# A modulation matrix on the matrix engine, retention scores of two heads in one go, and roots spread by row tiles

## The chip, the core and the metric

The kernel runs on one core of a Trainium2 chip. Five engines work side by side, each with its own queue of instructions, and meet at semaphores: TensorE (PE, with its weight loads shown as PEld), VectorE (DVE), ScalarE (ACT), GpSimd (POOL) and SyncE (SP), which here only issues transfers. 16 DMA engines move the data. The metric is the device time of the core in microseconds (us), as the median of repeated runs.

## The reference

Two transformer blocks are run on one sequence of 256 tokens with 1024 features, all in float32. What matters here:

```python
# block 1
mod = silu(c) @ w_ada + b_ada                      # c: 1024, w_ada: 1024 x 6144
sh1, sc1, g1, sh2, sc2, g2 = mod                   # six rows of 1024
h = rms_norm(x, norm1_g) * (1.0 + sc1) + sh1
u_val, u_gate, q, k, v, f_logit, gate_c, gate_a = split(h @ w_in)
conv_out = conv_module(u_val, u_gate, ...)         # 31 taps over time, 512 channels
attn = forgetting_attention(q, k, v, f_logit)      # uses cumsum(log_sigmoid(f_logit))
...                                                # mix, then 32 experts, 4 a token
# block 2, two layers
q_a, k_a, v_a, q_r, k_r, v_r, g_f, g_b, gate_logits = split(x @ w_in_2)
y_attn = windowed_gqa(q_a, k_a, v_a) @ w_o_attn    # 8 heads
# retention, 8 heads, key size 32, value size 64, forward and backward in time
y_ret = (silu(g_f) * head_norm(y_f) + silu(g_b) * head_norm(y_b)) @ w_o_ret
merged = sigmoid(g1) * y_attn + sigmoid(g2) * y_ret
...                                                # layer 0: dense FFN, layer 1: 8 experts
```

`head_norm` takes mean and variance over the 64 values of each head and direction, so a token has 16 roots per layer.

## The kernel before

Everything on the chip is kept with features on the 128 partitions and the 256 tokens (T) along the free side: `X` and `H` are 8 tiles (KT) of 128 x 256. `Z` (38 tiles of T columns), `SQ` and `SCR` (the end of `W`) are scratch. PSUM has 8 banks of 512 float32, `ps(b, ...)` is a part of bank b.

Weights come through a stream of slots of 1 MB each (`plan`, L70 to 125): in block 1 a ring of 15 buffers. SP issues the slots in the order of the stream (L444) and waits before each until the buffer's former content is used. `Linear` names a matrix and its number of slots; `lin_done` counts its finished groups, `job_evac` says which engine copies a job's result out of PSUM. Jobs use banks 0 and 1 in turn, and a job waits until the job two before it is copied out (`bank_free`).

The opening. ACT issues the small loads, then the tokens `x`. PE turns the tokens by transposes (L767), ACT squares them into `XSQ` (L1407) and copies them into `X` (L1409); PE sums the squares over the features with eight matmuls by a matrix of ones (L774); DVE and ACT make the root from it. Meanwhile DVE makes the modulation: for each of the eight slots of `ada0` (one slot is 128 rows of `w_ada` by 2048 columns) it multiplies the slot by the column `CSIL[:, s]` and adds it to `ADA` (`ada_products`, L1780 and L1783). PE then sums `ADA` over its partitions, with 16 matmuls of one column (`ada`, L724), and DVE adds the bias into `MOD` (L1788). DVE makes the gain `GS` and the modulated `H` in four pairs of tiles, `h_ready`. Then PE runs the projections `uqkv_a` (4 jobs) and `uqkv_b` (6 jobs), L662 and L714, with `ada(1)` between them, then the forget logits (L795) and `ada(2)`. In the stream two slots of `ada1` or `ada2` follow each of the first eight projection slots. ACT copies the projections out (L1432); ahead of that it issues four small loads (L1421 to L1424: forget weights, two routers, forget bias), of which PE's forget job waits for all. DVE makes the products of `ada1`, then `CONV_IN` and the first 15 of the 31 taps of the convolution (L1833, L1836) behind the products of `ada2`, then the log-sigmoid and running sum of the forget logits, `NEGF` (L1849). PE's jobs of the projection `gates` are each followed by attention scores (`scores1`, L814 to L823), which need `NEGF`, and DVE does the other 16 taps two at a time between them.

A layer's gate stage in block 2 (`mixer2`). Weights and inputs are split in two parts, hi and lo, which ACT (L396) and POOL (L400) make; a job is three passes, 96 instructions (L651). There are 12 gate jobs `gg`. After each of the first eight, PE does one head's share of the other work: in even steps the attention scores of two heads (`scores2`, L1178), in every step the retention scores of one head (`ret_scores`, L1190), then values and transposes (L1204, L843, L832). A head's retention keys and queries take 32 partitions, so each of its matmuls uses one row tile of the array; its bank is 2. ACT copies the gate job out (L1579, from the fifth on L1602), makes the decay factors and the exponentials, copies the transposed probabilities and splits a slot of weights. DVE weights the retention scores with the decay (L2219, `ret_weighted`).

After the gate jobs comes the head norm: sums by head (`head_sums`, L1233), the squares' sums into 16 rows by `HEADROW` (L1245), the 16 roots, and their spread over the 64 values of each head by `SPREAD` (L1255), which POOL builds (L596 to L600) once the last retention head is weighted. DVE multiplies bank by bank (L2255) and adds both directions (L2257).

The lines that the steps of the argument turn on:

```python
for name, n, ada in (("uqkv_a", 4, "ada1"), ("uqkv_b", 6, "ada2")):      # stream
    for s in range(n):
        stream.append((name, s))
        stream += [(ada, k) for k in range(min(2 * s, 8), min(2 * s + 2, 8))]
...
pe.wait_ge(sem("negf_ready"), 1)                                         # scores1(0)
...
def bank_free(job):
    if job >= 2:
        e, c = job_evac[job - 2]
        pe.wait_ge(sem("evac_" + e), c)
```

## Time and profile before

| | |
|---|---|
| median of 3 runs | 2409.09 us (2408.94 to 2410.05) |
| profiled execution, its own time | 2402.67 us |
| profiled execution, span | 2400.7 us |
| PE busy | 2273.2 us, 95% of the span |
| DVE, ACT, POOL busy | 735.9, 621.7, 385.2 us |

An engine's busy time is the time in which it worked on at least one instruction. A float32 matmul is two instructions in the trace. In a timeline a row with "x64" stands for 64 instructions, one after the other, with the time from the first one's start to the last one's end. In brackets stands the idle time of the engine before them and what ended it. ACTq and SPq are the queues of ACT and SP while they issue transfers. PEclk is the granted clock of PE as a share of its full speed, 2.4 GHz; its other level is 1.2 GHz.

### The profile page before, as it was taken

The page shows a single profiled execution, that of the slowest core. Times are in us where ns is not written, and L with a number is a line of the kernel's source. Part 1 is how long each engine was busy: PE and PEld are TensorE (multiplying, and loading weights), DVE is VectorE, ACT ScalarE, POOL GpSimd, SP SyncE. Part 2 cuts the span into 40 slices and gives each one's busy share as a digit, 9 for nine tenths or more (in the row PEclk, how much of TensorE's full clock was granted, in tenths as well). Part 3 has the DMA queues.
Part 4 walks back from the last instruction along what each step waited for, and adds up shares of the span by engine and source line. Part 5 has one row for each costly group of instructions (what it writes and reads, how often), then busy time and mean ns, then how long its engine had stood idle before and what let it go on. Part 6 is the DMA issues. An engine that isn't in the chain of part 4 may idle for free.

```text
span 2400.7 us, 34716 instructions
## 1 busy us (share of the span) xinstructions
PE 2273.2 (95%) x13090; PEld 1407.5 (59%) x13091; DVE 735.9 (31%) x1369; ACT 621.7 (26%) x901; POOL 385.2 (16%) x355
## 2 busy tenths in 40 slices
PE   5999899999999999999997999999999989999897
PEld 4887744444444444444446988899898863333333
DVE  6854322222222222222235234312314341111013
ACT  1143111111111111111214761443368011111111
POOL 1000000000000000000004741688486000000000
PEclk8999899999999999999998999999999989999999
DMA  9962389999999999989993433565454366999651
GB/s 371 370 233 101 95 341 418 418 418 417 418 417 418 417 418 417 418 341 414 418 393 106 158 106 105 163 190 180 119 176 124 122 249 260 362 405 396 278 234 72
DMA packets 226472, 688.61 MB, mean 287 GB/s; under 512 B 31386, under 2 KB 120418, under 8 KB 190562
## 3 DMA queue, kind: packets, MB, share of 16 engines
q1 hardware_dynamic: 221776, 685.82, 74.5%
q10 hardware_dynamic: 4626, 1.81, 0.3%
q8 instruction: 50, 0.82, 0.1%
q14 instruction: 20, 0.16, 0.0%
HBM read 686.53 MB, written 1.05 MB: 286 GB/s over the span
## 4 chain that ended last, share of the span: by engine, by line
PE 73%; DMA 10%; SPq 8%; DVE 4%; issue 1%; ACT 1%; ACTq 1%; POOL 0%; DVEq 0%; POOLq 0%
PE PS L992 16%; PE PS L651 12%; PE PS L662 11%; DMA RAW<-in_w_exp_in 9%; PE PS L1094 7%; SPq L453 6%; PE PS L1105 4%; PE PS L956 4%; PE PS L1287 3%; PE PS L975 2%; PE PS L706 1%; PE PS L748 1%; SPq L475 1%; PE PS L1003 1%; PE PS L1052 1%
## 5 line engine op out<-in xcount | busy, mean ns | idle before, releaser
L992 PE MATMUL PS<-RAW,Z 128*64 128x512 f32 x3168 | 713.7, 597 | 23.2 <-DMA RAW<-in_w_exp_in 23.2
L400 POOL TENSOR_TENSOR WLO_D<-W,WHI_D 128x512 fp32r<-128x512 f32 x284 | 361.8, 1310 | 1193.1 <-ACT WHI_D L396 1164.3
L992 PEld LDWEIGHTS PS<-RAW,Z 128*64 128x64 f32 x3168 | 213.7, 137 | 454.4 <-issue 376.7
L1094 PE MATMUL PS<-W,Z 128*64 128x512 f32 (+1 forms) x1056 | 212.8, 558 | 11.3 <-DMA W<-in_moe_w 10.6
L662 PE MATMUL PS<-Z,W 128*128 128x256 f32 x768 | 172.2, 385 | 2.1 <-DVE Z L1900 1.5
L396 ACT ACTIVATE WHI_D<-W 128x2048 fp32r<-128x2048 f32 x71 | 135.3, 1908 | 119.4 <-DMA W<-in_ffn_w 47.6
L1094 PEld LDWEIGHTS PS<-W,Z 128*64 128x64 f32 x1056 | 75.1, 137 | 149.1 <-issue 128.2
L662 PEld LDWEIGHTS PS<-Z,W 128*128 128x128 f32 x768 | 147.6, 193 | 25.2 <-DVE Z L1900 1.9
L956 PE MATMUL PS<-Z 128*128 128x64 f32 x1088 | 128.6, 278 | 0.0
L956 PEld LDWEIGHTS PS<-Z 128*128 128x128 f32 x1088 | 127.4, 196 | 0.3 <-issue 0.3
L2021 DVE TENSOR_TENSOR Z<-Z,PS 128x1024 f32<-128x1024 f32 x66 | 80.4, 1218 | 125.9 <-PE PS L975 125.9
L662 PE MATMUL PS<-H,W 128*128 128x256 f32 x512 | 116.1, 388 | 2.4 <-ACT Z L1432 2.4
L1515 ACT ACTIVATE Z<-PS 128x512 f32<-128x512 f32 x33 | 19.7, 597 | 367.1 <-PE PS L992 367.1
L651 PE MATMUL PS<-XHI,WHI_D 128*128 128x256 f32 x784 | 111.7, 285 | 1.4 <-POOL WLO_D L400 1.4
L1105 PE MATMUL PS<-W,Z 128*64 128x512 f32 x484 | 111.1, 599 | 0.0
L651 PE MATMUL PS<-XHI,WLO_D 128*128 128x256 f32 x784 | 110.1, 283 | 0.0
L651 PE MATMUL PS<-XLO,WHI_D 128*128 128x256 f32 x784 | 110.0, 283 | 0.0
L2047 DVE COPY Z<-PS 128x512 f32<-128x512 f32 x33 | 22.8, 692 | 280.0 <-PE PS L992 280.0
L662 PEld LDWEIGHTS PS<-H,W 128*128 128x128 f32 x512 | 98.8, 195 | 16.6 <-issue 2.9
L651 PEld LDWEIGHTS PS<-XHI,WHI_D 128*128 128x128 f32 x784 | 100.7, 191 | 3.1 <-POOL WLO_D L400 2.0
L651 PEld LDWEIGHTS PS<-XLO,WHI_D 128*128 128x128 f32 x784 | 101.1, 192 | 0.0
L651 PEld LDWEIGHTS PS<-XHI,WLO_D 128*128 128x128 f32 x784 | 101.1, 192 | 0.0
(384 smaller groups left out, 2333.8 us busy)
## 6 DMA issues: line engine op xcount, KB each, us to landing
RAW<-in_w_exp_in SPq DMA_DIRECT2D x256, 1024.0 KB, 19.3
RAW<-in_w_exp_out SPq DMA_DIRECT2D x128, 1024.0 KB, 21.8
W<-in_moe_w SPq DMA_DIRECT2D x128, 704.0 KB, 15.8
W<-in_w_in SPq DMA_DIRECT2D x52, 1024.0 KB, 5.9
W<-in_moe_w SPq DMA_DIRECT2D x40, 1024.0 KB, 16.1
W<-in_ffn_w SPq DMA_DIRECT2D x33, 1024.0 KB, 5.3
W<-in_w_ada SPq DMA_DIRECT2D x24, 1024.0 KB, 14.0
W<-in_w_out SPq DMA_DIRECT2D x12, 1024.0 KB, 5.1
```

Of the source, the lines that this page charges most:

```text
L396: eng.activation(hi, raw, ACT.Copy).then_inc(sem("dense_hi"), 1)
L400: i = eng.tensor_tensor(lo[:, c:c + 512], raw[:, c:c + 512], hi[:, c:c + 512].bitcast(F32), ALU.subtract)
L453: sp.dma_start(dst, src).then_inc(sem(f"raw{s}"), 16)
L651: mm = pe.matmul(ps(job % 2, T, c0=j * T), w[:, k, c:c + P], xp[:, k, :], start=(i == k == 0), stop=(i == 2 and k == KT - 1))
L662: mm = pe.matmul(ps(job % 2, T, c0=j * T), w[:, k, c:c + P], x[:, k, :], start=(k == 0), stop=(k == nk - 1))
L956: mm = pe.matmul(ps(2, HALF, c0=k * HALF), HT[:, a, k * P:(k + 1) * P], PICK[:, a, 0:HALF], start=(a == 0), stop=(a == 1))
L975: mm = pe.matmul(ps(6 + h, T, c0=j * T), YS1[64 * h:64 * h + 64, c:c + P], GT[64 * h:64 * h + 64, :], start=True, stop=True)
L992: mm = pe.matmul(ps(bank, 512, 64 * h, 64 * h + 64), x, w[:, c:c + 512], start=first, stop=final, skip_group_check=True)
L1094: mm = pe.matmul(o if b < 2 else o.rearrange("p (i n) -> p i n", i=2), X1[:, s, :], rhs, start=(s == 0), stop=(s == 7), skip_group_check=True)
L1105: mm = pe.matmul(ps(3, 512, 64 * h, 64 * h + 64), x, second2(j)[:, c:c + 512], start=(i == j == 0), stop=(j == 5), skip_group_check=True)
L1287: mm = pe.matmul(ps(j // 2, T, c0=(j % 2) * T), w[a][:, i, j * P:(j + 1) * P], x[:, i, :], start=(s == n == i == 0 and j % 2 == 0), stop=( ...
L2021: dve.tensor_tensor(o, o, PS[:, 6:8, :].rearrange("p h (k t) -> p h k t", k=2), ALU.add)\
```

## The change

1. The order of the stream and the split of the projections: `uqkv_a` has 6 slots and jobs, `uqkv_b` 4. One slot of `ada1` follows each of the first four projection slots, two each the next two; the slots of `ada2` follow the last four, two each.
2. `ada0` is multiplied on PE: for each slot four matmuls with `CSIL[:, s]`, broadcast to 32 columns, as weights, each into its own 32 partitions of bank 0 (four column tiles). DVE copies the result to SBUF, PE turns it with four transposes, DVE adds the bias. DVE's products of `ada0` go.
3. DVE first adds the eight squared tiles to two, and PE sums these with two matmuls into bank 3 instead of eight into bank 4.
4. The four small loads are issued by POOL, not ACT.
5. DVE does seven taps before `ada(1)` and eight after the products of `ada2`.
6. Gate jobs 0 to 8 all use one bank, so each from the second on waits for the copy of the job just before it. The freed bank holds the retention scores of the odd heads, and a pair's scores are computed together, in two row tiles, in the even steps. Job 9 waits until all heads are weighted.
7. `HEADROW` has 128 columns, so that the 16 sums (and roots) stand four times, at partitions 0, 32, 64 and 96. The spread runs in four row tiles at once, in two rounds. POOL builds `SPREAD` for all four with eight selects instead of two.

```diff
-    for name, n, ada in (("uqkv_a", 4, "ada1"), ("uqkv_b", 6, "ada2")):
-        for s in range(n):
+    for name, ada, upto in (("uqkv_a", "ada1", (1, 2, 3, 4, 6, 8)), ("uqkv_b", "ada2", (2, 4, 6, 8))):
+        for s, k in enumerate(upto):
             stream.append((name, s))
-            stream += [(ada, k) for k in range(min(2 * s, 8), min(2 * s + 2, 8))]
+            stream += [(ada, i) for i in range(upto[s - 1] if s else 0, k)]
...
+        def gate_bank(l, i):
+            return (lins[f"gg{l}"].job0 + (0 if i <= 8 else i)) % 2
...
+            pool.dma_start(WF, w_in[0][:, 5 * CW:5 * CW + HEADS].rearrange("(k p) n -> p k n", p=P)).then_inc(sem("ld_small"), 16)
...
-                for half in range(2):
-                    i = pool.affine_select(out=spread[:, :, half, :], in_=spread[:, :, half, :], compare_op=ALU.not_equal,
-                                           fill=1.0, base=-half, pattern=[[-2, KT], [0, HD]], channel_multiplier=1)
+                for r in range(4):
+                    for half in range(2):
+                        o = spread[32 * r:32 * r + 32, :, half, :]
+                        i = pool.affine_select(out=o, in_=o, compare_op=ALU.not_equal,
+                                               fill=1.0, base=-half, pattern=[[-2, KT], [0, HD]], channel_multiplier=1)
...
+            def gate_job(l, i):
+                lin = lins[f"gg{l}"]
+                q = split_ready(lin, i)
+                if 1 <= i <= 8:
+                    pe.wait_ge(sem("evac_act"), job_evac[lin.job0 + i - 1][1])
+                else:
+                    bank_free(lin.job0 + i)
+                    if i == 9:
+                        pe.wait_ge(sem("ret_weighted"), HEADS * (l + 1))
+                for j in range(2):
+                    for n, (w, xp) in enumerate(PASSES):
+                        w = w[:, q % SPLIT_N, :].rearrange("p (k n) -> p k n", k=KT)
+                        for k in range(KT):
+                            mm = pe.matmul(ps(gate_bank(l, i), T, c0=j * T), w[:, k, j * P:(j + 1) * P], xp[:, k, :],
+                                           start=(n == k == 0), stop=(n == 2 and k == KT - 1))
+                mm.then_inc(sem("lin_done"), 1)
...
+            def ada_rows(s):
+                w = weights(lins["ada0"].at[s])
+                for c in range(4):
+                    mm = pe.matmul(ps(0, 512, 32 * c, 32 * c + 32), CSIL[:, s:s + 1].broadcast_to([P, 32]),
+                                   w[:, 512 * c:512 * c + 512], start=(s == 0), stop=(s == 7),
+                                   tile_position=(0, 32 * c), skip_group_check=True)
+                mm.then_inc(sem("ada_used"), 1)
+
+            pe.wait_ge(sem("cond_ready"), 1)
+            for s in range(2):
+                ada_rows(s)
             pe.wait_ge(sem("ld_x"), 16)
...
+            for s in range(2, 4):
+                ada_rows(s)
+            pe.wait_ge(sem("x_sq"), 5)
+            for k in range(2):
+                mm = pe.matmul(ps(3, T), ONES[:, :], XSQ[:, k, :], start=(k == 0), stop=(k == 1))
             mm.then_inc(sem("x_squares"), 1)
-            ada(0)
+            for s in range(4, 8):
+                ada_rows(s)
+            pe.wait_ge(sem("ada_row"), 1)
+            for j in range(4):
+                tr = pe.transpose(ps(1, P, c0=j * P), ADA[:, j * P:(j + 1) * P], IDENT[:, :])
+            tr.then_inc(sem("lin_done"), 1)
...
-                def ret_scores(h):
-                    r = (h % 4) * RK
-                    n = HEADS * l + h
+                def ret_scores(h0):
+                    n = HEADS * l + h0
                     if n:
                         pe.wait_ge(sem("ret_weighted"), n)
                     for a in range(2):
-                        k0, q0 = (KR + h // 4) * T + a * P, (QR + h // 4) * T
-                        mm = pe.matmul(ps(2, T, c0=a * T), Z[r:r + RK, k0:k0 + P], Z[r:r + RK, q0:q0 + T],
-                                       start=True, stop=True, tile_position=(r, 0))
-                    mm.then_inc(sem("ret_scores"), 1)
+                        for h in (h0, h0 + 1):
+                            r = (h % 4) * RK
+                            k0, q0 = (KR + h // 4) * T + a * P, (QR + h // 4) * T
+                            mm = pe.matmul(ps(2 if h == h0 else gate_bank(l, 9), T, c0=a * T), Z[r:r + RK, k0:k0 + P],
+                                           Z[r:r + RK, q0:q0 + T], start=True, stop=True, tile_position=(r, 0))
+                            if a:
+                                mm.then_inc(sem("ret_scores"), 1)
...
-                for b in (0, 2, 1, 3):
-                    for k in (2 * b, 2 * b + 1):
-                        mm = pe.matmul(ps(4 + b, T, c0=(k - 2 * b) * T), SPREAD[:, k, :], SQ[0:16, 0:T], start=True, stop=True)
-                    mm.then_inc(sem("norm_sum"), 1)
+                for i in range(2):
+                    for r, b in enumerate((0, 2, 1, 3)):
+                        g = slice(32 * r, 32 * r + 32)
+                        mm = pe.matmul(ps(4 + b, T, c0=i * T), SPREAD[g, 2 * b + i, :], SQ[g, 0:T], start=True, stop=True,
+                                       tile_position=(32 * r, 0))
+                        if i:
+                            mm.then_inc(sem("norm_sum"), 1)
...
-            act.dma_start(WF, w_in[0][:, 5 * CW:5 * CW + HEADS].rearrange("(k p) n -> p k n", p=P)).then_inc(sem("ld_small"), 16)
...
-            dve.wait_ge(sem("cond_ready"), 1)
-            ada_products(0, 0, 6)
+            for p in (0, 2):
+                dve.wait_ge(sem("x_sq"), p + 2)
+                i = dve.tensor_tensor(pair(XSQ, p), pair(XSQ, p), pair(XSQ, p + 1), ALU.add)
+            link(i)
+            dve.tensor_tensor(pair(XSQ, 0), pair(XSQ, 0), pair(XSQ, 2), ALU.add).then_inc(sem("x_sq"), 1)
...
+            dve.wait_ge(sem("ada_used"), 8)
+            dve.tensor_copy(ADA[:, 0:512], ps(0)).then_inc(sem("ada_row"), 1)
...
             ada_products(1)
-            ada(1)
...
+            taps(7)
+            ada(1)
             ada_products(2)
-            taps(15)
+            taps(8)
```

## Rows read from the trace of the kernel before

**Rows 1.** Page, part 1: busy us, share of the span, instructions.

```profile
PE 2273.2 (95%) x13090; PEld 1407.5 (59%) x13091; DVE 735.9 (31%) x1369; ACT 621.7 (26%) x901; POOL 385.2 (16%) x355
```

**Rows 2.** Timeline of the opening, 17 to 76 us: start, us, engine, line.

```profile
17.71 2.07 ACT L1407 ACTIVATE Z<-PS 128x512 f32<-128x512 f32 x4 [6.93 <-issue]
...
34.83 6.99 PE L724 MATMUL PS<-ONES,Z 128*128 128x1 f32 x32 [6.83 <-DVE Z L1783]
...
41.92 0.17 DVE L1788 TENSOR_TENSOR MOD<-PS,VEC 128x16 f32<-128x16 f32 x1 [4.95 <-PE PS L724]
...
43.72 15.86 PE L662 MATMUL PS<-H,W 128*128 128x256 f32 x64
...
55.01 6.19 ACTq L1424 DMA_DIRECT2D BFG<-in_b_forget  x1
...
61.98 14.05 PE L662 MATMUL PS<-H,W 128*128 128x256 f32 x64 [2.41 <-ACT Z L1432]
```

**Rows 3.** Busy time by window, with granted clock, DMA share and GB/s.

```profile
5.00:145.00 140.00, 118.06 (x551) 101.00 (x552) 104.17 (x157) 24.50 (x41) 5.93 (x14) 0.90 1.06 375
...
208.00:212.00 4.00, 3.81 (x11) 2.87 (x11) 0.47 (x1) 0.15 (x1) 0.00 (x0) 0.60 0.00 0
...
1344.00:1440.00 96.00, 96.00 (x765) 86.06 (x764) 37.62 (x101) 73.00 (x133) 53.73 (x57) 1.00 0.38 114
```

**Rows 4.** Single slot transfers, issued at 12.7, 53.1 and 86.7, with time to landing.

```profile
DMA to landing us min/median/max: 17.2/17.2/17.2
...
L444 SPq DMA_DIRECT2D W<-in_w_ada x1: 6543/6543/6543, 53.1 to 53.1; - x1
...
DMA to landing us min/median/max: 17.3/17.3/17.3
...
L444 SPq DMA_DIRECT2D W<-in_w_in x1: 7357/7357/7357, 86.7 to 86.7; - x1
...
DMA to landing us min/median/max: 16.5/16.5/16.5
```

**Rows 5.** Timeline from 82 to 137 us: DVE's last products to the first scores.

```profile
82.40 17.13 DVE L1783 SCALAR_TENSOR_TENSOR Z<-W,CSIL,Z 128x2048 f32<-128x2048 f32 x7
...
100.73 22.25 DVE L1836 SCALAR_TENSOR_TENSOR Z<-W,VEC,Z 128x256 f32<-128x256 f32 x56
...
125.13 0.41 DVE L1688 SCALAR_TENSOR_TENSOR SQ<-SQ 8x256 f32<-8x256 f32 x1 [2.15 <-ACT SQ L1436]
...
135.59 0.28 DVE L1849 TENSOR_SCALAR W<-SQ 8x256 f32<-8x256 f32 x1
...
136.89 0.49 PE L814 MATMUL PS<-Z 64*128 64x128 f32 x4
```

**Rows 6.** Timeline of layer 0's gate stage: copies, scores of both kinds.

```profile
1357.99 0.60 ACT L1579 ACTIVATE Z<-PS 128x512 f32<-128x512 f32 x1 [0.59 <-PE PS L651]
...
1365.27 1.13 PE L1178 MATMUL PS<-Z 64*128 64x256 f32 x8
...
1365.95 0.60 ACT L1579 ACTIVATE Z<-PS 128x512 f32<-128x512 f32 x1
...
1375.18 1.13 PE L1190 MATMUL PS<-Z 32*128 32x256 f32 x4
...
1375.29 0.60 ACT L1579 ACTIVATE Z<-PS 128x512 f32<-128x512 f32 x1
...
1401.89 1.13 PE L1178 MATMUL PS<-Z 64*128 64x256 f32 x8
```

**Rows 7.** Line L932, four row tiles: ns min/median/max, first and last start.

```profile
L932 PE MATMUL PS<-Z,W x16: 629/629/792, 303.8 to 305.3; 32*128 32x256 f32 x16
```

**Rows 8.** Timeline of PE at 207 us, after a wait.

```profile
207.88 3.61 PE L732 MATMUL PS<-Z,ONES 128*128 128x256 f32 x8 [2.81 <-DVE GS L1879]
```

**Rows 9.** Timeline of the end of layer 0's retention: POOL's selects, spread.

```profile
1424.98 1.27 POOL L599 TENSOR_SCALAR_AFFINE_SELECT W<-W 16x512 f32<-16x512 f32 x2
...
1461.72 3.72 PE L1255 MATMUL PS<-SQ,W 16*128 16x256 f32 x16
```

More of the change, by code:

```diff
@@ L70, in plan @@
 def plan():
-    order = [Linear("ada0", 8, 1, "dve", 1), Linear("uqkv_a", 4, 1, "act"),
-             Linear("ada1", 8, 1, "dve", 1), Linear("uqkv_b", 6, 1, "act"), Linear("forget", 0, 1, "act"),
+    order = [Linear("ada0", 8, 1, "dve", 1), Linear("uqkv_a", 6, 1, "act"),
+             Linear("ada1", 8, 1, "dve", 1), Linear("uqkv_b", 4, 1, "act"), Linear("forget", 0, 1, "act"),
              Linear("ada2", 8, 1, "dve", 1), Linear("gates", 8, 1, "act"),
@@ L331, in transfers @@
             if name.startswith("uqkv"):
-                return cols(w_in[0], 256 * (s + (4 if name == "uqkv_b" else 0)), 256, buf)
+                return cols(w_in[0], 256 * (s + (6 if name == "uqkv_b" else 0)), 256, buf)
             if name == "gates":
@@ L1576, in mixer2, with copy @@
             def mixer2(l):
-                def copy(lin, s, dst, f=ACT.Copy, part=0):
-                    b = linear_ready(lin, s, part)
+                def copy(lin, s, dst, f=ACT.Copy, part=0, b=None):
+                    ready = linear_ready(lin, s, part)
+                    b = ready if b is None else b
                     act.activation(dst, ps2(b), f).then_inc(sem("evac_act"), 1)
@@ L1596, in mixer2 @@
                     if i < 4:
-                        copy(lin, i, z(GF + 2 * i, GF + 2 * i + 2), ACT.Silu)
+                        copy(lin, i, z(GF + 2 * i, GF + 2 * i + 2), ACT.Silu, b=gate_bank(l, i))
                     else:
-                        b = linear_ready(lin, i)
+                        linear_ready(lin, i)
+                        b = gate_bank(l, i)
                         for j in range(2):
```

63 lines of the change are left out of this document (32 added, 31 removed).

## Prediction

> **What bounds the kernel now.** I read the page first. PE is busy for 95% of the span [rows 1], so a microsecond counts only if it comes off PE's own chain, or off a wait in which PE stands. So I went to the two stretches that the change touches, the opening (0 to 140 us) and the retention stage of each layer (1344 to 1440 and 1776 to 1872 us), in order of time.
>
> In the opening the reader is to see that three things wait for one another. DVE makes the modulation sums, PE's column sums L724 start at 34.83 when the last is ready, the sums are back on DVE at 41.92, and the first projection starts at 43.72 [rows 2]. PE then waits 2.41 us for ACT, which stood in its own queue issuing small loads until 61.2 [rows 2]. And the 16 DMA engines are full (share 1.06) from 5 to 145 us [rows 3]: the landing of a slot of the stream is fixed by its place in it, not by who asks for it. Its 8th slot lands at 12.7+17.2 = 29.9, its 22nd at 53.1+17.3 = 70.4, its 34th at 86.7+16.5 = 103.2 [rows 4]. At the end of the opening PE's first scores L814 start at 136.89, 1.0 us after DVE's NEGF (L1849, 135.59+0.28) [rows 5]. So DVE is nearly the bound at that point already.
>
> In the retention stage PE is busy 96.0 of 96 us [rows 3] and goes from gate job to gate job, a pair in 18.3 us (36.62/2 between the scores at 1365.27 and 1401.89), and ACT is close behind it [rows 6].
>
> **The change, part by part.** *Start of the projections.* The eight row products on PE are 4 matmuls, 8 instructions of 512 columns, each. The nearest row for four tiles side by side is L932 in row tiles: 16 instructions started within 1.5 us, about 100 ns apart, though each lasted 629 ns [rows 7]. That is four abreast at 256 columns; 512 columns double it, so 8 instructions take 0.85 us at full and 1.7 at half clock if column tiles behave alike. The bound on the other side is no overlap: 3.4 and 6.8 us. I take four abreast, the nearest row. Then slot 7's product ends at 31 to 31.7; copy to SBUF, four transposes, MOD, gains and the first affine add about 3, and PE's own transposes L780 and L783 run beside them, since 41.92 to 43.72 was the like [rows 2]. The first projection starts near 34 to 35 instead of 43.72: 9 us earlier. The x squares are ready before that: ACT squares from 17.71 to 19.78 [rows 2], three additions, two matmuls, root, reciprocal and the product with X end near 28.
>
> *The small loads on POOL.* They leave ACT, so the 2.41 us go. POOL has nothing else to do there, and the loads are read some 60 us later; if POOL took 60 us over them, PE would wait for them.
>
> PE alone would now reach the scores at about 34.5+93.2-2.4-1 = 124.3 (93.2 is 136.89-43.72; the first 64 instructions took 15.86 us, the next 64 took 14.05 [rows 2], and of this cold start I let 1 us return): a gain of 12.6.
>
> *DVE up to the scores.* DVE's work is the same except the taps, and here the landings decide. The last slot of ada1 is now 22nd in the stream (it was 20th) and lands at about 70.6. Its product takes 2.45 (17.13/7) and ends at 73.0, CONV_IN 1.2, seven taps 28 x 0.397 (22.25/56) = 11.1, MOD 0.2: 85.6 [rows 5]. The products of ada2 would end at 85.6+1.3+17.1 = 104, but the last slots land at 100.6 and 103.2, so 105.6. Eight more taps are 32 x 0.397 = 12.7: 118.3. Then the log-sigmoid, which took 125.13 to 135.87 with 1.3 us of table load that is now done earlier: 9.5 to 10.7, so NEGF at 128.0 to 129.0 [rows 5]. PE reaches the scores at 128.7, not 124.3. Before, the forget logits came at 125.1, after the taps' end at 122.98, so the taps were hidden; with PE 12 us earlier this cover is gone. What is left of 12.6 is 136.9-128.7 = 8.2.
>
> PE stands still for about 4.5 us in front of the scores. After a 2.81 us wait L732 took 3.61 us, and the granted clock in 208 to 212 was 0.60: (1-0.60)/0.5, 80% of these 4 us, at the lower level of 1.2 GHz, which loses 1.6 us of work [rows 3, 8]. The scores and the start of the next gate job would lose as much or, after a longer wait, up to 2.5; I take 2.0, with 0 as the bound below, since no row is of such a wait behind projection jobs. So the opening gives 8.2-2.0 = 6.2. Both ends: 0 (the matrix work is not overlapped, below) and 12.6 (PE is never held).
>
> The Trainium skill, TensorE: Matmul & The Clock Gate, section Why this matters for your kernels, advises against such pauses between bursts of matmuls; by that rule the whole loss is due, and the trace agrees. By it the sum stays as it is; without it the opening would give 8.2.
>
> From 137 on nothing but PE's progress releases work: later loads wait for freed slots, and in the first expert stage, which runs on DMA, the stream starts from PE's progress also. So the gain is carried through at full size.
>
> *Two heads' retention scores.* Now each head has its own 4 instructions in one row tile, 1.13 us busy, while the attention scores with 8 instructions in two row tiles take the same 1.13 [rows 6]. So a pair costs what one head did: the odd steps lose about 1.05 us each, four per layer. The bound on the other side is no overlap, gain 0.
>
> *One bank for gate jobs 0 to 8.* Each job now waits for ACT's copy of the job before. Behind that wait on PE's queue are the next gate job and all scores and values after it. After an even job PE does 4 us of other work, which hides the copy. After job 1 only the transposes are left (0.4 us), and the copy ends 0.9 us after the job: 0.4 of the 1.05 goes. After jobs 3, 5 and 7 values and transposes take 1.45, the copy 0.9: hidden if ACT is on time. ACT's copies were at 1357.99, 1365.95 and 1375.29: 7.96 and 9.34 us apart, of which 0.7 idle, so ACT can do a pair in 16.6, and PE's pair goes from 18.3 to 17.25 [rows 6]. ACT keeps up, with 0.6 us a pair to spare. So 4 x 1.05-0.4 = 3.8 per layer, 7.6 in all.
>
> The Trainium skill (TensorEngine Tiling, section PSUM Bottleneck) says that tiling does not speed up the copies out of PSUM, which may become the bound: this is the third rival below.
>
> *Spread of roots.* Sixteen instructions (3.72 us) become four abreast, but DVE, which works on the results, could start 1.1 us after L1255 before, and can now too; its waits between banks were 0.2 to 0.4 [rows 9]. 0.3 per layer, 0.6 in all, bounds 0 and 1. HEADROW with 128 columns keeps its count of instructions: nothing. POOL's selects go from 2 to 8 at 0.63 (1.27/2) each, 3.8 us more, beginning 37 us before PE reads them [rows 9]: hidden; without that cover it would cost 3.8 a layer.
>
> **Sum.** 6.2+7.6+0.6 = 14.4 us. The profiled execution took 2402.67 (span 2400.7 and 2 around it), 0.27% below the median 2409.09; off the median that is 2394.7, or 0.60% faster.
>
> **Rivals.** *PE is not held at the scores* (the landings come earlier, or DVE is quicker): the opening gives up to 12.6, total 12.6+8.2 = 20.8, 2388.3. For it: PE's own sum. Against it: three landings and the fixed taps behind them. A half-way case, in which only the clock loss stays out, gives 16.4, 2392.7. Together 0.27. Forecast 0.40.
>
> *The 32-column tiles do not overlap, or the retention pairs do not.* For: no row shows 32-column tiles. At 3.4 us a slot at full clock PE is behind the stream, slot 7 is done near 40 and the first projection starts near 44 to 45; DVE's products of ada1 still end with the landing of slot 22, so the scores come at 130 to 134, and the gain is 3 to 7; with serial pairs the 7.6 go. Total 3 to 10, 2399 to 2406; centre 2402. Chance 0.23.
>
> *ACT becomes the bound of the gate jobs*, which ends on the other side. If the copy is over 0.55 us later than I have it after an odd job, PE stands. ACT's margin is 0.6 a pair; with a table load of 1.3 us more in each of 16 steps on the single-bank path PE loses 16 x 1.3 = 21 us, against 14.4+ gained: 2416. It turns slower once ACT's steps are above 0.9 us longer. Against: ACT's work is not changed. Chance 0.06. That nothing moves (gains and new waits cancel) has 0.04.
>
> **How the numbers follow.** Likeliest 2394.7, its own range 2391 to 2398. The 8-in-10 range leaves out half of the full-gain end and the last 0.1 on the slow side: 2388 to 2403. A change under 0.2% (4.8 us) can't be told from none: faster means under 2404.3. Faster 0.87 (0.40+0.27+0.20), same 0.08, slower 0.05.
>
> **What would show it.** The first projection (L662, H) at 34 to 35; ACT's first copies not late; DVE's last product of ada2 at 105 to 106; an idle gap of 3 to 5 us on PE with DVE's NEGF as releaser, scores at 128 to 129, then lower clock. In the retention stage, gate jobs 5.8 us long with 17.2 to 17.3 us for a pair, and a wait on ACT of about 0.4 after job 1 alone. Wrong if the 22nd and 34th slots land elsewhere, if 8 instructions of the row product take over 2 us, or if ACT's copies release most gate jobs.

## The result, and the profile after

The changed kernel takes 2387.32 us (median of 4 runs, 2382.27 to 2387.82) against 2409.02 for the kernel before, taken again beside it (2405.69 to 2410.05): ratio 0.9912, 95% interval 0.9900 to 0.9924, 21.7 us. The prediction was 2394.7 with a range down to 2388.0: the right direction, and the time lies 0.7 us outside the range.

The two profiled executions differ by less. The changed kernel's took 2387.82 (span 2386.1), that of before 2402.67: 14.85 us, where the sum said 14.4. So the traces agree with the sum and the medians don't agree with the traces. The agreement of the first is partly luck: at the job `attn_out`, behind the opening, the two profiles are 7.7 us apart where the sum had 6.2, and 6.9 come behind it where the sum had 8.2. The gap of 7 us between traces and medians is what most of the experiments are about.

The page of the kernel after, part 1 (busy us, share of the span, instructions), to be set beside [rows 1]:

```profile
PE 2259.8 (95%) x13114; PEld 1391.4 (58%) x13115; DVE 729.7 (31%) x1365; ACT 621.8 (26%) x901; POOL 395.5 (17%) x371
```

PE is as full as before and 13.4 us shorter: nearly the whole gain between the two profiles is work or low clock taken off PE. The timeline of PE in the opening of the kernel after (start, us, engine, line):

```profile
28.40 1.06 PE L798 MATMUL PS<-W,CSIL 128*32 128x512 f32 x8 [1.76 <-DMA W<-in_w_ada]
...
32.34 41.68 PE L691 MATMUL PS<-H,W 128*128 128x256 f32 x192 [0.32 <-DVE H L1770]
```

Eight row-product instructions of 512 columns take 1.06 us from first start to last end, so the 32-column tiles do run four abreast, where the prediction had 0.85, and PE waits 1.76 us for the slot to land. The first projection starts at 32.34, where [rows 2] has 43.72. The two rows that stopped PE in [rows 2] are gone: POOL issues the four small loads in half to one us each, and ACT's first copy is on time. POOL, then ACT:

```profile
36.80 1.09 POOL L581 DMA_DIRECT2D W<-in_w_in  x1
37.88 0.91 POOL L582 DMA_DIRECT2D WR<-in_w_router  x1
38.78 0.88 POOL L583 DMA_DIRECT2D WR<-in_router_w  x1
39.65 0.54 POOL L584 DMA_DIRECT2D BFG<-in_b_forget  x1
```

```profile
39.52 0.60 ACT L1481 ACTIVATE Z<-PS 128x512 f32<-128x512 f32 x1 [3.69 <-PE PS L691]
```

The timeline of the end of the opening, beside [rows 5]:

```profile
102.05 2.35 DVE L1834 SCALAR_TENSOR_TENSOR Z<-W,CSIL,Z 128x2048 f32<-128x2048 f32 x1 [0.27 <-DMA W<-in_w_ada]
...
104.31 12.75 DVE L1893 SCALAR_TENSOR_TENSOR Z<-W,VEC,Z 128x256 f32<-128x256 f32 x32
...
116.98 0.41 DVE L1739 SCALAR_TENSOR_TENSOR SQ<-SQ 8x256 f32<-8x256 f32 x1
...
126.91 0.28 DVE L1908 TENSOR_SCALAR W<-SQ 8x256 f32<-8x256 f32 x1
...
127.33 0.80 PE L862 MATMUL PS<-Z 64*128 64x128 f32 x4 [4.53 <-DVE W L1908]
```

DVE waits for the landing of the last slot of ada2, makes eight taps, and NEGF is ready at 127.2. PE has stood for 4.53 us and starts the scores at 127.33, 9.6 us earlier than in [rows 5]; its first four instructions take 0.80 where [rows 5] has 0.49. The layer 0 gate stage, beside [rows 6]:

```profile
1350.94 1.18 PE L665 MATMUL PS<-XHI,WHI_D 128*128 128x256 f32 x8 [0.34 <-ACT Z L1629]
...
1356.85 1.13 PE L1226 MATMUL PS<-Z 64*128 64x256 f32 x8
1357.91 1.13 PE L1241 MATMUL PS<-Z 32*128 32x256 f32 x8
...
1368.20 1.19 PE L665 MATMUL PS<-XHI,WHI_D 128*128 128x256 f32 x8
```

Two heads' retention scores take the 1.13 us that one head's took in [rows 6], this pair of jobs takes 1368.20-1350.94 = 17.26 us, and after job 1 the profile names ACT as what released job 2. It names no other, yet the next two pairs take 17.50 us each. PE and ACT between jobs 5 and 6:

```profile
1385.05 0.66 PE L880 MATMUL PS<-IDENT,SQ 128*128 128x128 f32 x4
1385.70 1.19 PE L665 MATMUL PS<-XHI,WHI_D 128*128 128x256 f32 x8
```

```profile
1384.72 0.84 ACT L1653 ACTIVATE Z<-PS,VEC 128x256 f32<-128x256 f32 x2
```

The job starts 0.65 us after the transposes begin, where jobs 3, 4 and 5 start 0.41 to 0.43 after theirs, and 0.14 us after ACT's copy ends, as job 2 does (1350.94, its copy ends at 1350.80). Job 8 starts 0.65 behind its transposes too. From the fifth job on ACT copies out in two pieces, 0.84 us and not 0.60, and its copies of jobs 5 and 7 begin 17.50 us apart, as PE's pairs do. So in these pairs ACT's copy, and not PE's own work, is what releases a job, at a price of 0.24 us each. The windows of the kernel after (us, busy time of each engine, granted clock, DMA share, GB/s) that answer to [rows 3], and one over the scores:

```profile
5.00:145.00 140.00, 123.38 (x611) 98.86 (x612) 93.89 (x165) 29.07 (x49) 9.23 (x18) 0.95 1.06 375
...
127.00:131.00 4.00, 3.67 (x16) 2.82 (x16) 0.27 (x2) 0.00 (x0) 0.00 (x0) 0.50 1.05 387
```

The DMA engines are full as before. The granted clock over the scores is 0.50, the lower level of 1.2 GHz throughout.

### The profile page after: what moved, and what is told of

Same layout as the page of the kernel before. It is cut to its first block, busy times and chain, and to the rows that moved or that the text cites. A ratio compares the mean times of both kernels' runs of the same rounds, so it can differ in the third digit from the quotient of the medians.

```text
span 2386.1 us, 34777 instructions
## 1 busy us (share of the span) xinstructions
PE 2259.8 (95%) x13114; PEld 1391.4 (58%) x13115; DVE 729.7 (31%) x1365; ACT 621.8 (26%) x901; POOL 395.5 (17%) x371
## 4 chain that ended last, share of the span: by engine, by line
PE 67%; DMA 13%; SPq 11%; DVE 6%; issue 2%; ACT 1%; POOL 0%; ACTq 0%; DVEq 0%; POOLq 0%
PE PS L1040 16%; DMA RAW<-in_w_exp_in 9%; PE PS L691 9%; SPq L458 7%; PE PS L1142 6%; PE PS L680 6%; PE PS L665 6%; PE PS L1004 4%; PE PS L1153 3%; PE PS L1342 3%; SPq L480 3%; DMA W<-in_w_ada 3%; PE PS L1023 2%; PE PS L735 1%; PE PS L777 1%
## 5 line engine op out<-in xcount | busy, mean ns | idle before, releaser
L1040 PE MATMUL PS<-RAW,Z 128*64 128x512 f32 x3168 | 713.6, 597 | 23.2 <-DMA RAW<-in_w_exp_in 23.1
L691 PE MATMUL PS<-Z,W 128*128 128x256 f32 x768 | 170.5, 382 | 7.3 <-DVE Z L2317 5.8
L691 PEld LDWEIGHTS PS<-Z,W 128*128 128x128 f32 x768 | 146.7, 192 | 29.4 <-issue 5.1
L1142 PEld LDWEIGHTS PS<-W,Z 128*64 128x64 f32 x1056 | 75.1, 138 | 151.3 <-issue 131.9
L2080 DVE TENSOR_TENSOR Z<-Z,PS 128x1024 f32<-128x1024 f32 x66 | 80.4, 1218 | 125.9 <-PE PS L1023 125.9
L691 PE MATMUL PS<-H,W 128*128 128x256 f32 x512 | 115.5, 387 | 0.3 <-DVE H L1770 0.3
L691 PEld LDWEIGHTS PS<-H,W 128*128 128x128 f32 x512 | 98.7, 194 | 14.1 <-DMA W<-in_w_in 0.4
L2183 DVE TENSOR_TENSOR Z<-PS,Z 128x512 f32<-128x512 f32 (+1 forms) x22 | 10.5, 520 | 255.7 <-ACT Z L1599 255.7
L1571 ACT ACTIVATE SQ<-PS 128x512 f32<-128x512 f32 x33 | 19.7, 597 | 248.7 <-PE PS L1040 248.7
L2069 DVE TENSOR_SCALAR Z<-Z,SQ 128x128 f32 x66 | 19.9, 344 | 207.7 <-PE PS L1013 207.7
L1023 PEld LDWEIGHTS PS<-Z,SQ 64*128 64x128 f32 x536 | 46.1, 186 | 57.4 <-issue 54.5
L1023 PE MATMUL PS<-Z,SQ 64*128 64x256 f32 x536 | 76.0, 402 | 0.7 <-ACT Z L1550 0.7
L1153 PEld LDWEIGHTS PS<-W,Z 128*64 128x64 f32 x484 | 31.8, 136 | 57.6 <-issue 57.6
## 6 DMA issues: line engine op xcount, KB each, us to landing
RAW<-in_w_exp_out SPq DMA_DIRECT2D x128, 1024.0 KB, 21.7
W<-in_w_ada SPq DMA_DIRECT2D x24, 1024.0 KB, 14.6
```

Source lines behind the costliest of these rows:

```text
L691: mm = pe.matmul(ps(job % 2, T, c0=j * T), w[:, k, c:c + P], x[:, k, :], start=(k == 0), stop=(k == nk - 1))
L1023: mm = pe.matmul(ps(6 + h, T, c0=j * T), YS1[64 * h:64 * h + 64, c:c + P], GT[64 * h:64 * h + 64, :], start=True, stop=True)
L1040: mm = pe.matmul(ps(bank, 512, 64 * h, 64 * h + 64), x, w[:, c:c + 512], start=first, stop=final, skip_group_check=True)
L1142: mm = pe.matmul(o if b < 2 else o.rearrange("p (i n) -> p i n", i=2), X1[:, s, :], rhs, start=(s == 0), stop=(s == 7), skip_group_check=True)
L1153: mm = pe.matmul(ps(3, 512, 64 * h, 64 * h + 64), x, second2(j)[:, c:c + 512], start=(i == j == 0), stop=(j == 5), skip_group_check=True)
L2080: dve.tensor_tensor(o, o, PS[:, 6:8, :].rearrange("p h (k t) -> p h k t", k=2), ALU.add)\
```

## The experiments

Each kernel ran beside the kernel before, both on one chip. There were four batches of such runs, on three chips in all; each ratio is taken within a batch, and times from two batches are less comparable. A gain in us is worked out from the ratio, except where two medians are given.

**The kernel before, again.**

> The kernel before once more, for its spread. The profiled execution of before took 2402.67 us while its timed runs took 2405.7 to 2410, so the gain is 14.9 us between the two profiled executions and 21.7 between the medians. Theory A (the granted clock after waits returns at another moment in every execution): the new profile differs from the old one by some us, in stages behind a wait of PE (the norms, the routing, the start of the experts) and with another clock there; the opening up to 128 us is equal within 0.5 us. Theory B (the small loads that ACT issues stand longer in most executions than the 2.4 us of the first profile): the new profile shows PE waiting 5 us or more for ACT near 60 us.

2406.14 us, ratio 0.9999 (0.9991 to 1.0008). Its profiled execution took 2402.39 and lies within 0.7 us of the first all the way. So the profile repeats, and it sits 4 us under its own median again. Neither theory's sign came: the low clock stood in the same places, and PE waited 2.58 us for ACT, not 5.

**Only the four small loads on POOL's queue.**

```diff
+            pool.dma_start(WF, ...)      # and WR1, WR2, BFG
-            act.dma_start(WF, ...)       # and WR1, WR2, BFG
```

> The kernel before with the four small loads issued by POOL and nothing else changed. Theory A: PE's wait of 2.4 us near 60 us is gone and the scores start 2.4 us earlier, or later than that only as far as DVE's log-sigmoid chain holds them (NEGF came 1.0 us before PE needed it, and it hangs on the forget logits, which come earlier too): 2.0 to 2.6 us faster in time. Theory B: 6 to 9 us faster in time.

2404.91, ratio 0.9988 (0.9979 to 0.9998): 2.7 us between the medians, the size of the wait in [rows 2]. The interval ends at 5.1 us and so leaves out theory B's 6 to 9. The trace shows 2.9 us at `ada(1)`, and then a loss of clock in the projections and in `ada(2)` that gives them back: the scores start at 137.28. The twelve executions spread from 2397.7 (mean granted clock 0.978) to 2408.2 (0.970).

**The whole opening, without the retention stage's part.** The loads, the row products, the stream's new order and the taps.

> The whole opening (stream order, row products on PE, fewer sums of squares, loads on POOL, taps split), the retention stage and spread as before. Theory A: first projection at 32.3, NEGF as releaser of the scores at 127.3, a gain of 7.6 us once the scores are done, 7 to 8.5 in time. Theory B: the gain in time is 12 to 15 us, since the long stand on ACT goes too.

2396.02, ratio 0.9954 (0.9941 to 0.9966): 11.1 us (8.2 to 14.2), where the sum had 6.2. That is more than theory A's 7 to 8.5 and less than theory B's 12 to 15. NEGF was no releaser here: PE came to the scores by itself at 127.33, after it had lost clock in its projections, and ran them at full clock.

**Only the retention pairs and the single bank.**

```diff
-                    ret_scores(i)                   # one head, every step
+                    if i % 2 == 0: ret_scores(i)    # heads i and i+1, two banks
```

> The pair of retention scores and the single bank for gate jobs 0 to 8, all else as before. Theory A: a pair of gate jobs takes 17.2 us instead of 18.3, 3.6 us per layer, so 7.2 us faster in time, plus or minus 1.5 for the clock's phase. Rival (ACT is late for the single bank): PE waits for ACT after most odd jobs, gain under 4 us. Theory B says nothing else here.

2399.38, ratio 0.9972 (0.9960 to 0.9983): 6.7 us (4.1 to 9.6; the medians differ by 8.2), where the sum had 7.6. In the trace the stage gives 3.3 us in each layer.

**Only the spread of the roots by row tiles,** with its tables.

> The kernel before with only the spread of the roots by row tiles, with its tables. The opening part gave 11.1 us timed and the retention pairs 6.7 us, and the whole change 21 to 22: 3 to 4 us are neither's. Theory A (the three parts add by their traces, 0.3 us a layer for the spread, and the rest is the clock's moment of return, another one in each execution): the trace shows 0.3 us at each spread and the timed gain is 0 to 1.5 us. Rival: the spread is where the missing 3 to 4 us are, since the short matmuls that it does away with hold the clock down: a timed gain of 3 us or more, and a stretch of higher clock behind each spread.

2404.00 against 2407.27, ratio 0.9993 (0.9984 to 1.0002): not told from nothing. The interval reaches to 3.9 us, so the timing alone does not rule out the missing 3 to 4 us, but the trace shows nothing like it. The timeline of this kernel at the spread, beside [rows 9]:

```profile
1463.16 1.15 PE L1259 MATMUL PS<-SQ,W 32*128 32x256 f32 x16
1466.48 1.10 PE L664 MATMUL PS<-Z,W 128*128 128x256 f32 x4 [2.17 <-DVE Z L2263]
1468.31 6.96 PE L664 MATMUL PS<-Z,W 128*128 128x256 f32 x31 [0.73 <-DVE Z L2263]
```

The sixteen matmuls fell from 3.72 to 1.15 us, and 2.17 of the 2.57 saved came back as a wait for DVE. What is left is 0.6 us a layer over the whole head norm.

**The changed kernel, again.**

> The changed kernel once more, unaltered, for the spread of its executions. Theory A (the trace of the change adds up to 14 to 15 us, and what the timed runs give beyond that is where TensorE's clock stood low in each execution): the median stays at 2385 to 2388, single executions spread over 5 us or more, and the lower mean granted clocks carry the longer times. Theory B (the changed kernel has a saving of about 6 us that its one profile missed): the new profile's stage times differ from the first one's at a fixed place with equal clocks there.

2386.87 (2381.44 to 2387.74), ratio 0.9903 (0.9888 to 0.9919). The profile differs from the first mainly in places where the clock stood otherwise; besides, the last slot of `ada0` landed about 1 us later (PE's row products on it start at 29.37 and not at 28.40). One of the places is the start of the second expert stage. First the kernel after, then its second profile, each in the same window of the span:

```profile
1955.00:1980.00 25.00, 24.17 (x115) 9.03 (x117) 1.45 (x5) 2.50 (x5) 0.00 (x0) 0.88 0.75 299
```

```profile
1955.00:1980.00 25.00, 23.70 (x126) 9.24 (x127) 3.46 (x8) 3.32 (x6) 0.00 (x0) 1.00 0.80 322
```

At the same instructions the second is 2.9 us quicker here, while it lost as much some 70 us before, where the first had full clock (granted clock from 1880 to 1890: 1.00 in the first, 0.66 in the second).

**The four loads back on ACT,** in the changed kernel.

> The changed kernel with its four loads of whole rows back on ACT's queue. Theory A: they stand in front of ACT's copies of the first projections as the rows of before show, PE is held for about 3 us in the opening, and since DVE's log-sigmoid (bound by the landings) sets the first scores, most of that is inside the 4.5 us wait: 0 to 2 us slower than the changed kernel. Rival: the loads alone are worth 2.9 us wherever they stand: 3 us slower. Rival: the profiles don't show their real cost, and the runs without a profile have the loads standing for the 8 us that before's queue row reads: 6 us slower.

2387.39, ratio 0.9916 (0.9902 to 0.9930): 0.5 us from the changed kernel, inside the spread. ACT's queue and its first copies in this kernel:

```profile
42.37 3.42 ACTq L1475 DMA_DIRECT2D BFG<-in_b_forget  x1
45.83 0.60 ACT L1483 ACTIVATE Z<-PS 128x512 f32<-128x512 f32 x1 [9.79 <-issue]
46.64 0.60 ACT L1483 ACTIVATE Z<-PS 128x512 f32<-128x512 f32 x1 [0.21 <-PE PS L687]
```

The last load stood 3.42 us and not the 6.19 of [rows 2], and ACT was through just before job 2 needed it: with the projections at 32.5, the loads' place no longer mattered.

**Work in PE's wait at the scores.** 18 matmuls of constants and H into a free bank, which add nothing to the result.

> The changed kernel with 18 matmuls of 256 columns into a bank that is free, between the first gates job and the first scores, so that TensorE works where it waited 4.5 us. They add nothing to the computation. If the scores run at half clock because PE stood still before them, they now take 3.6 us and not 5.5: 1.5 to 2 us faster than the changed kernel. Rival: the scores' own short matmuls bring the clock down, or it was down since the one-column matmuls of ada(2): no change, or up to 0.5 us slower by the tail of the 18.

2388.01, ratio 0.9919 (0.9905 to 0.9932): no faster, where 1.5 to 2 us were expected. Each float32 matmul is two instructions, which I had not counted, so the filler took twice what I meant. The timeline of this kernel:

```profile
121.51 7.93 PE L903 MATMUL PS<-H,ONES 128*128 128x256 f32 x36
129.37 0.49 PE L862 MATMUL PS<-Z 64*128 64x128 f32 x4
```

The scores start 2.04 us later than in the kernel after and run at full clock: 129.37 to 132.92, 3.55 us, where the kernel after needs 127.33 to 132.83, 5.50. The loss of 1.95 us is thus tied to PE's standing, and the filler's overrun ate it.

**More taps behind the log-sigmoid.**

```diff
-            taps(8)                      # ahead of the log-sigmoid
+            taps(3)
...
-                    taps(2)              # in each score job
+                    taps(3 if i < 5 else 2)
```

> Twelve groups of four taps fewer ahead of the log-sigmoid: three k instead of eight before it, and three instead of two in each of the first five score jobs. By my account the wait of 4.5 us at the first scores is DVE's, so DVE reaches NEGF some 8 us earlier (5 x 4 x 0.40), PE doesn't wait there, and the clock isn't lowered after it: 4.5 to 6.4 us faster than the changed kernel, about 2381 to 2383. Rival: the four added taps of a job delay the normalisation of the probabilities, and PE's transposes of them then wait: 0 to 3 us faster only. Rival: evac_act for the queries or keys, and not NEGF, is late there by nearly as much: 0 to 1 us faster.

2384.54, ratio 0.9898 (0.9883 to 0.9913): 2.3 us under the changed kernel's second median, less than its spread, and not the 4.5 to 6.4 expected. The timeline shows a new limit:

```profile
115.08 0.41 DVE L1739 SCALAR_TENSOR_TENSOR SQ<-SQ 8x256 f32<-8x256 f32 x1 [5.92 <-ACT SQ L1485]
...
125.53 0.28 DVE L1908 TENSOR_SCALAR W<-SQ 8x256 f32<-8x256 f32 x1
...
126.84 0.49 PE L862 MATMUL PS<-Z 64*128 64x128 f32 x4
```

DVE now waits for the forget logits, so of the 8 us expected NEGF gains 1.4. NEGF is ready 1.0 us before PE comes, and PE doesn't wait: it came late by itself, since its first projection started at 35.73 in this execution and not at 32.34.

**32 columns instead of one in the sums of ada(1) and ada(2).**

```diff
-                    mm = pe.matmul(PS[:, bank, j:j + 1], ADA[...], ONES[:, 0:1])
+                    mm = pe.matmul(ps(bank, 32, c0=32 * j), ADA[...], ONES[:, 0:32])
```

> The changed kernel with the column matmuls of ada(1) and ada(2) taking 32 equal columns of ones and not one, so that each writes 32 equal columns (DVE reads one of them). If a matmul is bound by its weight load at 0.11 us either way, the 32 records still take 3.6 us. If it is the single column that lets the clock down behind them, the 32 records behind ada(2) take 7.0 us and not 8.84, and the 64 behind ada(1) 13.9 to 14.1: up to 1.8 us sooner at the end of the projections, which the wait for NEGF then hides, 0 to 2 us faster timed. Rival: the clock falls all the same, no change, or slower by what 32 columns add.

2388.18, ratio 0.9922 (0.9909 to 0.9935): no change. The 32 instructions took 3.76 us, as long as with one column, and behind `ada(2)` the clock fell all the same (8.84 us for a job that takes 7.1 at full clock):

```profile
109.39 3.76 PE L753 MATMUL PS<-ONES,Z 128*128 128x32 f32 x32
112.98 8.84 PE L691 MATMUL PS<-H,W 128*128 128x256 f32 x32
127.31 0.80 PE L862 MATMUL PS<-Z 64*128 64x128 f32 x4 [5.48 <-DVE W L1908]
```

Behind `ada(1)` it didn't fall here (7.15 and 7.14 us for the two jobs), and neither did it in the kernel with work in the wait at the scores, which has one column.

**Work in PE's waits behind the six norms,** alone and with the later taps.

```diff
+            for _ in range(20):
+                pe.matmul(ps(6, P), ONES[:, :], IDENT[:, :])   # behind the last sum of squares
```

> The changed kernel with 20 matmuls of 128 columns (a free bank, constants, nothing of the result) issued behind the last sum of squares of each of the six norms, where PE stands for 4.7 to 5.4 us and then runs at half clock. At 0.22 us each they end 0.4 us before the wait does. If the standing is what lowers the clock, the router's logits take 3.6 us each and not 7.0, its transposes 1.1 and not 1.95, the first jobs behind three norms save 1.7 to 3 us each, the second expert stage starts at full clock (0 to 4 us), and the end 0.5: 10 to 17 us faster than the changed kernel, 2370 to 2377, and a smaller spread of single executions. Rival: the clock's budget is spent over a longer stretch and the filled waits are taken back from the matmuls behind them: 0 to 3 us faster, with a lower clock in the expert stages. Rival: the fill outlasts the wait: slower by up to 1 us a norm.

> The same fills in the kernel with the taps moved behind the log-sigmoid, which alone was 2.3 to 2.8 us faster than the changed kernel: 12 to 20 us faster than the changed kernel, 2367 to 2375. Rival: the two overlap, since both gain from the same clock: no more than the fills alone.

2385.32 (2382.69 to 2392.89), ratio 0.9918 (0.9903 to 0.9933), and 2385.08, ratio 0.9902 (0.9888 to 0.9916). Neither is told from the changed kernel, though their mean granted clocks are 0.980 to 0.985 and those of the changed kernel 0.975 to 0.979: 10 to 17 and 12 to 20 us were expected, and the intervals leave no room for them. The fill does its work where the first wait is. At the first router of the filled kernel PE is busy up to the wait's end, and the logits take 4.13 us, not 7.04:

```profile
269.11 4.63 PE L759 MATMUL PS<-IDENT,ONES 128*128 128x128 f32 x40
273.95 4.13 PE L959 MATMUL PS<-WR,H 128*128 128x32 f32 x32 [0.21 <-ACT H L1533]
277.89 1.95 PE L952 MATMUL PS<-IDENT,H 128*128 128x128 f32 x8
```

But the transposes behind it are at half clock again (1.95 us, as without the fill). At the second router the logits, no longer slow, wait for ACT's four pieces instead:

```profile
1935.69 1.06 PE L959 MATMUL PS<-WR,X 128*128 128x8 f32 x8 [0.30 <-ACT X L1458]
```

And in front of the dense stage's third job, PE, now early, waits 2.00 us for POOL (0.52 in the kernel after) and then runs slow (1.75 and 1.91 us where 1.12 is the full-clock time):

```profile
1727.15 1.22 PE L680 MATMUL PS<-XHI,WHI_D 128*128 128x256 f32 x8 [2.00 <-POOL WLO_D L400]
1728.21 1.75 PE L680 MATMUL PS<-XHI,WLO_D 128*128 128x256 f32 x8
1729.76 1.91 PE L680 MATMUL PS<-XLO,WHI_D 128*128 128x256 f32 x8
```

**Further draws of both kernels.** These four runs ask whether a profiled execution is a draw like any other.

> The kernel before, a third profiled execution. The timed gain is 21 to 22 us and the gain between profiled executions 14.6 to 15.6, since both profiled executions of the kernel before (2402.7 and 2402.4) lie at the fast end of its 2402 to 2411. Theory A (a profiled execution is a draw like any other, and the draws differ by where the clock stood low): the third lies anywhere in 2402 to 2411, and where it is above 2405 its trace shows the extra time as steps of 1 to 4 us at waits or short matmuls with a lower granted clock there. Theory B (a profiled execution of this kernel isn't like an unprofiled one): 2402.5 within 1 us for a third time.

> As the third, a fourth draw. Under theory A the chance that four draws all lie within 1 us of the fast end is small; under theory B it is what happens.

> The changed kernel, a third profiled execution; the two before were 2387.8 and 2386.9 of a range 2381 to 2388. Theory A: anywhere in 2381 to 2388, a fast one without one of the steps at the sums per head of layer 1 (3.7 us) and at the start of the second expert stage (4.1 us), of which each of the first two profiles showed one. Theory B: 2387 within 1 us again.

> As the third, a fourth draw of the changed kernel, with the same two expectations.

The profiled executions of before took 2408.23 and 2409.34, those of the changed kernel 2385.99 and 2384.85. So four profiles do not all lie at the fast end, and theory B falls: the first two profiles of before lay at the short end of what it does. The third loses 5.4 of its 5.6 us in one place; the fourth is 4.6 us later than the first at the scores, 3.0 at `attn_out` and 6.7 at the end. The projections in the third profile of before, beside [rows 2]:

```profile
62.34 15.74 PE L662 MATMUL PS<-H,W 128*128 128x256 f32 x64 [3.68 <-ACT Z L1432]
77.92 4.69 PE L724 MATMUL PS<-ONES,Z 128*128 128x1 f32 x32
82.47 30.14 PE L662 MATMUL PS<-H,W 128*128 128x256 f32 x128
...
142.27 0.49 PE L814 MATMUL PS<-Z 64*128 64x128 f32 x4
```

and the windows of the same stretch:

```profile
62.00:78.00 16.00, 15.66 (x66) 13.53 (x66) 6.17 (x3) 2.57 (x4) 0.00 (x0) 0.89 1.08 380
78.00:82.50 4.50, 4.50 (x34) 4.50 (x32) 0.00 (x0) 0.60 (x1) 0.00 (x0) 0.75 1.09 385
82.50:112.00 29.50, 29.50 (x127) 25.62 (x128) 28.56 (x35) 1.79 (x3) 0.00 (x0) 0.92 1.07 368
```

After a wait of 3.68 us (2.41 in [rows 2]) the clock is below 1.00 in all three groups: 15.74 for 14.05, 4.69 for 3.63, 30.14 for 27.87. That is 5.0 us, and with the later start the scores come at 142.27, 5.4 later than in [rows 5]. The fourth profile of before has the same (15.74, 4.24, 30.61; scores at 141.51).

These two ran on another chip than the second, and there none of 31 executions of before took less than 2405.38 us, where 8 of 35 did in the second's batch. So the chip may have a part in it. The low clock is not that chip's alone: two of the experiments have the opening of before unchanged and ran on the two other chips. The one with only the spread starts its scores at 138.72, with 15.74 us in the first group. The one with only the retention pairs starts them at 139.30, after this:

```profile
75.81 4.26 PE L747 MATMUL PS<-ONES,Z 128*128 128x1 f32 x32
79.94 30.59 PE L685 MATMUL PS<-H,W 128*128 128x256 f32 x128
```

The mean of all six starts is 139.2, that of the four profiles 139.3. The changed kernel loses clock in these projections too, and it doesn't show. Its third and fourth profile at the scores:

```profile
127.49 0.49 PE L862 MATMUL PS<-Z 64*128 64x128 f32 x4 [2.83 <-DVE W L1908]
```

```profile
127.27 0.49 PE L862 MATMUL PS<-Z 64*128 64x128 f32 x4 [1.39 <-DVE W L1908]
```

The eight profiles, in us; the third column is the start of the first instruction of the job `attn_out` (L662 before, L691 after). What the last column's difference has over the third's came behind that job:

| kernel | scores start | `attn_out` starts | span |
|---|---|---|---|
| before, four profiles | 136.89, 136.67, 142.27, 141.51 | 215.89, 215.64, 221.34, 218.90 | 2400.7, 2400.4, 2406.3, 2407.4 |
| after, four profiles | 127.33, 128.92, 127.49, 127.27 | 208.16, 208.10, 206.32, 204.65 | 2386.1, 2385.1, 2384.2, 2383.1 |
| mean before less mean after | 11.6 | 11.1 | 19.1 |

The first two of each kernel alone are 8.7, 7.6 and 15.0 us apart, the last two of each, all four of one batch, 14.5, 14.6 and 23.2.

## Why the prediction was wrong

**What was right.** The first projection was put at 34 to 35; it starts at 32.34 to 35.11. Column tiles four abreast: 1.06 us for eight instructions at full clock, 0.85 predicted. Landings fixed by place: the last product of ada2 ends at 104.4, predicted 105.6. PE held by NEGF for 3 to 5 us with the scores at 128 to 129: 4.53 us and 127.33 in the first profile, though 0, 2.83 and 1.39 us in the others. The gate pair at 17.2 to 17.3: 17.26 for the first, with a wait on ACT of 0.34 after job 1, predicted 0.4. Nothing was serial, so the rival of tiles that do not overlap fell. The rival of ACT as the bound came true in small: 0.24 us for each of two pairs a layer.

**The retention stage and the spread.** 3.8 a layer was predicted for the pairs, 3.3 came. What is short is ACT's: its pair of 16.6 us was read off the copies of jobs 1 to 3, and from the fifth job on its copies are longer, so two pairs take 17.50 and not 17.26 (2 x 0.24 = 0.5). 0.3 was predicted for the spread, about 0.6 came, and not by the way given: DVE did not start as early as before, PE waited 2.17 us for it. Together 8.2 against 8.0 behind `attn_out` in the table's means (19.1-11.1). The overlap in row tiles stands; that the sum comes out so well is two small misses that offset each other.

**The step that failed is the opening's term, 8.2-2.0 = 6.2; it measured 11.1,** both timed alone and in the means of four profiles. It was mis-sized at both of its ends, and by one omission: it took the path of before from one profiled execution, 136.89 at the scores, as the kernel's. In the means, the 8.2 is 11.6 (2.4 from the scores of before at 139.3 and not 136.9, 1.0 from those of after at 127.8 and not 128.7), and the 2.0 is 0.5 (the difference falls from 11.6 at the scores to 11.1 at `attn_out`).

First, the path before. Between 62 and 113 us PE is alone on the path there, so each us of low clock in its projections moves the scores. The first profile had full clock all through; the third and fourth had not, and came 5.4 and 4.6 us later. The mean of the four is 139.3, not 136.9: 2.4 us more to gain.

Second, the path after. Here the landings and DVE set the scores, and PE's time of arrival can vary without moving them. PE would have come at 122.8, 128.9, 124.7 and 125.9 (start less wait), a spread of 6.1 us, and the scores start at 127.27 to 128.92, a spread of 1.7. The low clock that costs the kernel before 5 us is here hidden, in the main, behind the wait for NEGF. This I had put down as a limit that costs 4.4 us (PE held), without asking what else the slack would absorb.

Third, the 2.0 for low clock at the scores, which was charged in full. It came in one of four profiles (and in that of the kernel with 32 columns): where PE stood for 4.53 us the clock was 0.50 over the scores, and where it stood for 5.48 they took as long; where it stood for 2.83, 1.39 or not at all, the first four instructions took 0.49, as at full clock. The Trainium skill (TensorE: Matmul & The Clock Gate, section Part 1: The HAM clock gate) says that the moment at which the clock changes differs between runs of one kernel; the eight profiles agree, by up to 5 us in the opening and 2.9 at the start of the second expert stage. I cited the page for the loss and not for its variation.

Then the median. I took the sum off 2409.09 although the profile it was made from took 2402.67, and called the difference 0.27%. That 6.4 us was itself the sign that this profile was shorter than what the kernel usually does: time that the median has and the rows have not, in places unknown, some of it where the change works.

**What stays open.** The four profiles give 19.1 us, the timed medians 21 to 22. The last 2 to 3 us lie in executions without a profile. Of these 0.3 to 0.6 are outside the span: an execution takes 2.1 to 2.4 us more than its span in the kernel before, as the mean of a batch, and 1.7 to 1.8 in the changed one. The rest may be the mix alone, since the four profiles of the last batch give 23.2 and the four others 15.0; no run shows how often each kind of opening comes, or whether the chip decides it. Nor is it shown why the clock in before's projections falls in some executions. Both of the low ones follow a wait of 3.4 to 3.7 us for ACT, the high ones one of 2.4 and 2.6; but the kernel with the retention pairs alone lost clock from `ada(1)` on after a wait of 2.07, and the kernel with the loads alone, without any such wait, lost it in the projections behind `ada(1)`.

## What to carry to other kernels

A profile is one draw. When it lies away from the median, find out which draws the median is made of before a sum is made: more profiles of the kernel before would have put the start of the scores at 139 instead of 137. That takes 2.4 us off the forecast and its range, and 2387.3 lies inside 2385.6 to 2400.6.

When a change turns a stretch from bound by one engine to bound by transfers, its gain can be more than the difference of the two paths at full clock: the slack also swallows whatever made the old path vary. Price it with the usual execution, not with the shortest.

Filling a wait with dead matmuls to hold the clock pays only as far as the next producer allows. Here it took 2.9 us off the logits, and ACT's pieces, POOL's splits and the next fall of the clock took them back; the six fills together gave nothing that the timing could tell.

## What the runs showed of the hardware

Low clock moves from place to place between executions of one kernel. The changed kernel's first profile ran the second expert stage's start at 0.88 and the second at 1.00 (21.98 and 19.11 us for the same 96 instructions); in the kernel with the loads alone, mean clocks of 0.970 to 0.978 go with 2408 down to 2398 us.

Issuing a small load on ACT's queue has no fixed price: the forget bias took 6.19 us in the first profile of before, 7.89 and 8.14 in its third and fourth, and 3.42 when it came 12 us earlier, while POOL issued it in 0.54.

16 matmuls (32 instructions) by one column take 3.63 to 3.73 us at full clock, by 32 columns 3.65 and 3.76. In both cases the clock fell behind those of `ada(2)` (8.84 us for the next job and not 7.1), though not in every execution (7.15 in the kernel with the retention pairs alone).

A copy out of PSUM can hold PE without being named: the profile gives no idle time for gate jobs 6 and 8, and they start 0.24 us later behind their transposes than the others do.
